# The gate products of the two gated mixers run one weight tile ahead of the up products, with two places for the sigmoid and the merged rows' low halves in three pieces

## The reference, cut to what matters

```python
a = rms_norm(h, g_mix)
q, k, v, g_ret, cb, cc, ch, gate_r, gate_c = split(a @ w_in)
ret = silu(g_ret) * head_group_norm(chunkwise_retention(rotary(q), rotary(k), v))
y_ret = ret @ w_ret_up
z = causal_short_conv(cc * ch, conv_w, conv_b)
y_conv = (cb * z) @ w_conv_up
merged = sigmoid(gate_r) * y_ret + sigmoid(gate_c) * y_conv
h = h + merged @ w_out
h = h + peer_ffn(rms_norm(h, g_ffn), ...)     # queries, top-k of product keys, experts
ple = p @ w_ple_proj
h = h + sigmoid(rms_norm(h, g_ple) @ w_ple_gate) * ple
return rms_norm(h, g_final)
```

## Time and profile before

| what | value |
|---|---|
| time, median of 3 runs | 3687.8 us (3678.93 to 3694.53) |
| the profiled execution | 3681.89 us, of which the span is 3680.1 us |
| PE busy (matmul) | 3420.2 us, 93% |
| VectorE (DVE) busy | 2709.3 us, 74% |
| GpSimd (POOL) busy | 2170.0 us, 59% |
| ScalarE (ACT) busy | 1195.2 us, 32% |
| granted TensorE clock, mean | 0.966 |

### The profile page before, as it was taken

The page is one execution under the profiler, slowest core; times in us unless marked ns, Lnnn a source line. Parts: engine busy times, 40 slices in busy tenths (PEclk is TensorE's granted clock), DMA queues, the critical chain, the costliest instruction groups (busy, mean ns, idle before and its releaser), DMA issues. The chain is left out here.

```text
span 3680.1 us, 59182 instructions
## 1 busy us (share of the span) xinstructions
PE 3420.2 (93%) x22379; PEld 3353.9 (91%) x22379; DVE 2709.3 (74%) x4191; ACT 1195.2 (32%) x1855; POOL 2170.0 (59%) x1406
## 2 busy tenths in 40 slices
PE   7899978989999889899999999998999999989987
PEld 6799978989999789899999999997999999989965
DVE  5524368676886666998989898652888888888854
ACT  2310131232221233455656555542222222222232
POOL 5478755323687555566666666664666666656521
PEclk9999989999999899999999999998999999999998
DMA  4233322112688768788888888897988989979701
GB/s 150 81 114 122 130 97 69 61 48 74 230 312 304 257 217 280 250 314 291 314 293 307 305 307 308 320 345 248 316 307 304 315 314 317 323 267 325 244 18 63
DMA packets 324155, 851.86 MB, mean 231 GB/s; under 512 B 27536, under 2 KB 125328, under 8 KB 320656
## 3 DMA queue, kind: packets, MB, share of 16 engines
q0 software_dynamic: 110592, 402.70, 30.6%
q1 hardware_dynamic: 72864, 258.15, 20.5%
q10 hardware_dynamic: 140528, 188.78, 14.7%
HBM read 754.62 MB, written 94.90 MB: 231 GB/s over the span
## 5 line engine op out<-in xcount | busy, mean ns | idle before, releaser
L582 POOL TENSOR_TENSOR w_lo<-raw,w_hi 128x1024 fp32r<-128x1024 f32 x206 | 544.8, 2645 | 434.4 <-ACT w_hi L1017 430.6
L681 PE MATMUL main<-mix_hi,w_hi 128*128 128x320 f32 (+1 forms) x2816 | 689.9, 319 | 52.9 <-issue 17.1
L681 PE MATMUL main<-mix_lo,w_hi 128*128 128x320 f32 (+1 forms) x2816 | 677.2, 314 | 0.0
L681 PE MATMUL main<-mix_hi,w_lo 128*128 128x320 f32 (+1 forms) x2816 | 676.3, 314 | 0.0
L609 POOL DMA_INDIRECT rows<-v_rows,s_idx x384 | 391.4, 1019 | 335.2 <-DVE scr L1632 273.2
L681 PEld LDWEIGHTS main<-mix_hi,w_hi 128*128 128x128 f32 x2816 | 480.7, 191 | 57.8 <-issue 40.5
L1632 DVE SCALAR_TENSOR_TENSOR scr<-rows,s_dot,scr 128x1024 f32<-128x1024 f32 x381 | 487.9, 1281 | 45.1 <-DMA rows<-v_rows,s_idx 34.6
L926 PE MATMUL main<-h_hi,v_hi 128*128 128x320 f32 x2048 | 474.9, 313 | 38.0 <-DVE res L2022 20.8
L681 PE MATMUL main<-a_hi,w_hi 128*128 128x320 f32 (+1 forms) x1728 | 466.7, 324 | 34.4 <-POOL w_lo L582 18.2
L609 POOL DMA_INDIRECT rows<-u_rows,s_idx x384 | 390.2, 1016 | 162.3 <-DVE s_dot L1625 85.2
L681 PEld LDWEIGHTS main<-mix_lo,w_hi 128*128 128x128 f32 x2816 | 484.0, 191 | 0.0
(11 more groups left out here) (243 smaller groups left out, 5310.7 us busy)
## 6 DMA issues: line engine op xcount, KB each, us to landing
raw<-stream SPq DMA_DIRECT2D x474, 512.0 KB
act_d<-actb ACTq DMA_DIRECT2D x128, 320.0 KB
gate_d<-gbuf ACTq DMA_DIRECT2D x20, 2048.0 KB, 10.1
h<-act_d ACTq DMA_DIRECT2D x128, 320.0 KB
gate_in<-gate_d ACTq DMA_DIRECT2D x31, 1280.0 KB
rows<-u_rows,s_idx POOLq DMA_INDIRECT x384
rows<-v_rows,s_idx POOLq DMA_INDIRECT x384
score_d<-stage ACTq DMA_DIRECT2D x16, 320.0 KB
```

The lines of the kernel that those rows point to most:

```text
L582: pool.tensor_tensor(w_lo[:, s, :], raw[:, s, :], w_hi[:, s, :].bitcast(F32), ALU.subtract) \
L681: last = pe.matmul(main[s][:, dst:dst + n], wt[:, s, c * P:(c + 1) * P], rows[:, c, src:src + n], start=(c == 0 and wt is w_hi and rows is ...
```

## The change

The order of the 16 tiles of M1, and of M2, changes. Before, it was gate 0, up 0, gate 1, up 1 and so on. Now it is gate 0, gate 1, up 0, gate 2, up 1, ..., gate 7, up 6, up 7: gate n is tile 2n-1 (`gate_at`), up n is tile 2n+2 (`up_at`), but the last up is tile 15. The host lays the stream out so. All gates but the first go to `main[1]`, all ups but the last to `main[0]`. Since two sigmoids are alive at a time there is a second place, `sg_ahead`, by the parity of n. The loops of ScalarE and VectorE over the pairs are written out in pass 0 too. In M1 of pass 1 the exponentials of the sparse scores, the picks and the ranks keep their place between the pairs; `spare` is called one tile later in each pair. The low halves of the merged rows, seven in a row before the last merge until now, are made in pieces: rows 0 to 3 after gate 7 is done and before merge 6, rows 4 to 6 after merge 6, row 7 after merge 7. The casts of the high halves stay where they were in ScalarE's queue, behind all sigmoids and, in pass 1, behind the weight casts of M2.

```diff
@@ SBUF
-        nt0, rowb, sg, pbuf, z = [], [], [], [], []
+        nt0, rowb, sg, sgs, pbuf, z = [], [], [], [], [], []
...
+                ahead = lay(f"sg_ahead{k}", [P, w], F32)
+                sgs.append((sg[k], ahead))
@@ TensorE, mixers
-                of_mix(base + M1_PAIR, 1, ready=2 * DC * ps)
-                with pe.Fori(1, DC) as n:
-                    of_a(base + M1_PAIR + n, 0)
-                    of_mix(base + M1_PAIR + n, 1)
+                of_a(base + M1_PAIR, 1)
+                of_mix(base + M1_PAIR + 1, 0, ready=2 * DC * ps)
+                of_a(base + M1_PAIR + 1, 1)
+                with pe.Fori(2, DC - 1) as n:
+                    of_mix(base + M1_PAIR + n, 0)
+                    of_a(base + M1_PAIR + n, 1)
+                for s in range(2):
+                    of_mix(base + M1_PAIR + DC - 1, s)
...
                 of_a(base + M2_PAIR, 0)
+                of_a(base + M2_PAIR, 1)
                 pe.wait_ge(z_used, DC * ps + DC + 1)
-                of_mix(base + M2_PAIR, 1)
...
@@ ScalarE, mixers
-                def gate(tile, merged):
+                def gate(first, n, merged):
+                    tile = 2 * first + gate_at(n)
                     act.wait_ge(tile_done, tile + 1)
-                    act.wait_ge(merged_done, merged)
...
+                    act.wait_ge(merged_done, merged + max(n, 1))
+                    act.activation(alike(sgs[ps][n % 2][:, :], ps), cols(main[tile % 2], ps), ACT.Sigmoid) \
+                        .then_inc(main_drained[tile % 2], 1)
+
+                def gates(first, merged, between=lambda at: None):
+                    for at in range(2 * DC):
+                        if at == 0 or at % 2 and at < 2 * DC - 1:
+                            gate(first, (at + 1) // 2, merged)
+                        if ps:
+                            after(first + at // 2, at % 2)
+                        between(at)
@@ VectorE, mixers
+                def up_product(first, n, out):
+
+                    g, u = 2 * first + gate_at(n), 2 * first + up_at(n)
+                    dve.wait_ge(main_drained[g % 2], g // 2 + 2)
+                    dve.wait_ge(tile_done, u + 1)
+                    dve.tensor_tensor(alike(out, ps), cols(main[u % 2], ps), alike(sgs[ps][n % 2][:, :], ps),
+                                      ALU.mult).then_inc(main_drained[u % 2], 1)
+                    dve.wait_ge(main_drained[u % 2], u // 2 + 2)
...
                 def merge(n):
...
+                    r, sgn = res_row(n, ps), sgs[ps][n % 2][:, :]
+                    if n < DC - 1:
+                        spare(2 * M2_PAIR + up_at(n) - 1)
+                    up_product(base + M2_PAIR, n, sgn)
+                    steps.then(dve.tensor_tensor(r, r, sgn, ALU.add))
                     dve.sem_inc(merged_done, 1)
...
+                    if n < DC - 2:
+                        spare(2 * M2_PAIR + up_at(n))
...
-                dve.wait_ge(tile_done, 2 * (base + M2_PAIR + DC - 1) + 1)
-                lo_of(ps, 2 * DC, a_lo[ps], a_hi[ps], range(DC - 1))
+                for n in range(DC - 2):
+                    merge(n)
+                dve.wait_ge(tile_done, 2 * (base + M2_PAIR) + gate_at(DC - 1) + 1)
+                lo_of(ps, 2 * DC, a_lo[ps], a_hi[ps], range(4))
+                merge(DC - 2)
+                lo_of(ps, 2 * DC, a_lo[ps], a_hi[ps], range(4, DC - 1))
                 merge(DC - 1)
@@ host
-    for n in range(DC):
-        parts += [gc[n], up_c[n]]
+    parts += ahead(gc, up_c)
```

More of the change, by code:

```diff
@@ L132, in tile_of, with gate_at, up_at @@
     return LEAD + SPAN * (m // 16) + QUARTERS[m % 16]
+def gate_at(n):
+    return 2 * n - 1 if n else 0
+def up_at(n):
+    return min(2 * n + 2, 2 * DC - 1)
 def row_homes():
@@ L1138, in mixers @@
                         act.copy(row_of(mix_hi[ps], 2 * i + k), z[ps][:, :]).then_inc(z_hi, 1)
-                with act.Fori(0, DC) as n:
-                    gate(2 * (base + M2_PAIR + n), done + 2 * DC + n + 1)
-                    if ps:
-                        for s in range(2):
-                            after(base + M2_PAIR + n, s)
+                gates(base + M2_PAIR, done + 2 * DC)
                 for c in range(DC):
@@ L1836, in mixers @@
                 if ps == 0:
-                    with dve.Fori(0, DC) as n:
+                    for n in range(DC):
                         gated(n)
@@ L1844, in mixers @@
                         steps.leave(inside, DC // 2)
-                    with dve.Fori(0, DC - 1) as n:
-                        inside = steps.enter(n, 1)
-                        merge(n)
-                        steps.leave(inside, DC - 1)
                 else:
```

63 lines of the change are left out of this document (20 added, 43 removed).

## The result

The changed kernel takes 3697.1 us, median of 20 runs, against 3687.2 us for 20 runs of before: a ratio of 1.0028, 95% interval 1.0019 to 1.0037. The sign is right, and so is the forecast that the two kernels lie within 0.5% of each other.

The account below looks back on a forecast made before the run. PE, busy 93% of the span, bounds the kernel, so only edges count: 0 + 1.9 + 0.3 - 0.4 + 5.8 - 1 = +6.6 us on 3687.8 gives 3694.4 us, range 3682 to 3703.

Parts of the forecast that it names:

- What bounds the kernel: PE works 93% of the span; nothing to win inside M1 and M2, so the change acts at the edges only.
- M1 begins, pass 0: Start of M1, pass 0: wait for `mix_lo` becomes a like wait for the sigmoid; 0 us, bounds -2.3 and +1.4.
- it ends at 186.09 + 0.49 = 186.58: M1, pass 0: end of gate 0's sigmoid, so up 0 starts 2.1 us later than before.
- M1 begins, pass 1: Start of M1, pass 1: idle joins into one wait of about 7 us, then lower clock; +1.9 us, bounds 0 and +2.
- C begins, pass 1: Start of C, pass 1: last pick and `s_idx` late, partly covered; +0.3 us, bounds 0 and +1.3.
- M2, pass 0: Pass 0: convolution wait at M2's start goes, -0.4 us; M2's end gains little as VectorE and GpSimd take turns, -1.
- M2 ends, pass 1: End of M2, pass 1: low halves wait for `a_hi`, three dots and merge 6 follow; +5.8 us, bounds +5.2 and +8.
- (a): Rival: low-half pieces work in both passes, last `a_hi` casts 5.2 and 5 us earlier; 3679.4 us, chance 0.1.
- (b): Rival: the loss at M2's end in pass 1 is hidden in the `x_t` loads; 3688.6 us, chance 0.1.
- (c): Rival: gather ring stops GpSimd inside M2 too, up to 3 us for each of six merges; 3712 us, chance 0.05.

Follow-up runs that it names:

- held kernels: GpSimd's two halves of M1's fourth tile, pass 0, held until row 6's cast: changed kernel 3691.48 us (single execution); with all edges 3663.25 us.
- piece of seven: Changed kernel with pass 1's low halves in one piece again, behind merge 6; pass 0 keeps its pieces: 3688.24 us, ratio 1.0002.
- all edges: Changed kernel, pass 1: three dots before low halves, row casts early, M1's first weight cast and sigmoid early, dots before `x_t` wait: 3665.75 us, ratio 0.9947.
- empty hold: GpSimd's halves of M1's fourth tile, pass 0, held until row 4's cast, already made: changed kernel 3695.3 us; with all edges 3669.98 us.

## Why the prediction was right

**What bounds the kernel: right.** PE has no wait inside M1 or M2 in either pass; over 1116 to 1216 us of after it is busy without a gap. All that moved lies at the edges.

**M1 begins, pass 0: forecast 0, measured +2.6; the step that failed.** The mechanism that I named is there: up 0 waits for the sigmoid (the profile calls it issue: PE starts at 191.37, 0.1 us after the sigmoid's end), and the matmuls behind it start at the lower level. What failed is "it ends at 186.09 + 0.49 = 186.58". I moved PE's tiles and let ScalarE's and VectorE's times stand. But gate 1 in up 0's place ends 7.7 us sooner and frees GpSimd's halves sooner, which meet VectorE's two `y`. I had reasoned just so at the end of M2 in pass 0, and did not ask it here. Its size is 3.89 - 1.03 = 2.9 us, and the held kernels give 3.0 back. PE was then at the lower level for 12 matmuls where I had counted 15, which took 0.4 us off. The upper bound of +1.4 did not hold the 2.6 us.

**M1 begins, pass 1: forecast +1.9, measured +2.55.** One wait of 6.78 us for w_lo, as laid out. PE starts at the lower level, 0.53 us from pair to pair in place of 0.29, for 11 pairs, where I had counted 9 and 2.0 us; 11 x 0.24 = 2.6. The term was mis-sized, the mechanism right. One part of it I had not seen: before, PE was at the lower level too after its first wait there, for 12 matmuls,

```profile
827.63 0.90 PE L681 MATMUL main<-mix_hi,w_hi 128*128 128x320 f32 x2 [2.53 <-DVE mix_lo L1657]
```

but the second wait, to 835.47, stood behind them and covered them. So PE's idle time was not only moved together; it grew from 5.1 to 6.8 us, since the tiles ahead of it now run fast, and what costs time is that the slow start now stands behind the last wait.

**C begins, pass 1: forecast +0.3, measured -0.1.** I had put `s_idx` at 1.5 to 3.3 us late, and that did not come: it is made 4.5 us behind the first copy of C, where it was 4.3, and the first gather follows at 5.8, where it was 5.6. The instruction that makes it takes 0.29 us, where it took 1.29 beside a low half on GpSimd; how the rest of the delay went is not worked out. PE has no wait there: the lower of my bounds.

```profile
952.36 1.11 POOL L621 DMA_INDIRECT rows<-u_rows,s_idx  x1 [1.65 <-DVEq L1615]
```

**M2, pass 0: forecast -0.4 and -1, measured -1.9.** The 0.4 us wait is gone. VectorE and GpSimd take turns as I had laid out:

```profile
413.80 5.04 DVE L1675 TENSOR_TENSOR a_lo<-res,a_hi 128x384 fp32r<-128x384 f32 x4 [3.58 <-ACT a_hi L1164]
418.76 0.55 DVE L1778 TENSOR_TENSOR sg<-main,sg 128x384 f32<-128x384 f32 x1
419.34 2.17 DVE L1834 TENSOR_TENSOR res<-res,sg 128x384 f32<-128x384 f32 x1
421.66 4.27 DVE L1675 TENSOR_TENSOR a_lo<-res,a_hi 128x384 fp32r<-128x384 f32 x3 [0.15 <-DVE res L1834]
```

Seven low halves take 9.3 us, where one piece took 8.58, and the add between them 2.17 in place of 0.56. From M2's first sigmoid to the last cast it is 427.08 - 357.81 = 69.3 us, before 423.49 - 353.46 = 70.0: -0.8. The other 1.1 us lie behind the last cast (39.3 us to the end of the stage before, 38.1 after): the 2.2 us wait for the first `add_out` went, since PE ran slow just where it would have waited. That 1.1 us is luck: with M1's old order the same code, with the clock up a little longer, has the wait again.

The Trainium skill (SBUF — State Buffer, "Who interferes with whom") makes the port pair that VectorE and GpSimd share an exclusive lock. The trace agrees: two products `y` go from 1.03 to 3.89 us, in pass 1 from 1.56 to 3.66. Of the seven low halves above, the three that meet no GpSimd instruction, or start just ahead of one, take 0.55 to 0.57 us, and the four that meet one 1.16 to 2.76, each until 0.4 us behind its end.

**M2 ends, pass 1: forecast +5.8, measured +6.9 for the stage and +6.0 from the last weight cast to the second tile of O.** Line by line: four low halves 3.03, dots to 1229.25, merge 6 with the add at 1.23 against a low half on GpSimd, three low halves 2.30, merge 7 ended 1235.37. That is 12.5 us from the first low half, and I had 12.2. Of the other 0.9 us of the stage 0.75 lie behind the start of the second tile of O (56.56 us to the end of the stage, before 55.81): PE is at the lower level for 21 steps there where it was for 15, though its wait is the shorter one. The slow start of the first tile costs nothing, as I had said, since the second wait stands behind it. That the whole piece of seven brings back the old stage shows what was added to the path; that the early casts take another 8.0 us off, on top of the dots, shows that ScalarE's queue held the pieces there.

**The rivals.** (a) is out in the change as it stands: the idle before the first low half is put down to `a_hi`, and with the casts moved, and the dots first, its pass 1 comes true. (b) is out: the wait for `x_t` is 9.14 us, it was 8.79. The loads moved with the cast by their full amount. (c) is out: no wait inside M2. That the sum came to +6.6 against +10.1 is the 2.6 us of M1 in pass 0, 1.1 at the end of M2 and 0.65 in M1 of pass 1, less 0.5 in pass 0 and 0.4 in C. That the forecast lies only 2.7 us off in time is in part luck: the medians differ from before's by 9.9 us in one measurement (20 runs of after) and by 5.4 in the other (12).

## What to carry to other kernels

When a step is moved between engines that work in order, go through the queue of every engine that feeds it, not only the one that was edited: here low halves were cut in pieces for VectorE while their casts stayed behind a weight cast on ScalarE, and the pieces put three dots and a merge on the path. Six casts moved two places forward, with the dots first, turned the same edit from a loss of 6.9 us in its stage into a gain of 6.5. And when a wait has independent work queued behind it, do that work first: one call ahead of a wait for loads gave the kernel before 10.8 us in that stage, without any reordering.

## What the runs showed of the hardware

A product or subtraction of VectorE with two operands in SBUF, 128x384, takes 0.55 us alone, 1.2 to 1.4 when it meets GpSimd's cast of a weight tile and 2.2 to 2.8 when it meets the subtraction. Which of them meet depends on which product ended first, so a change in PE's order can cost on engines that it doesn't name. Holding GpSimd back by 3.5 us gave 3.0 back.

PE starts a weight tile's matmuls at the lower level after a wait of 3.69 us, as after one of 15.6, but also after waits of 1.84, 2.19 and 2.53 us (before, at 421.45, 431.85 and 827.63). After 2.55 us (before, 835.47), 2.77 (one piece of seven) and 2.03 (all edges) it starts at the higher. A slow start costs nothing when another wait stands behind it, as at 827.63, and its full length behind the last one: 2.6 us in M1 of pass 1. After three waits of 0.20, 1.33 and 1.39 us (421.34 to 428.24) it fell in after and not with M1's old order, whose waits are the same to 0.01 us: what the engine waited did not alone decide it.

The parts of the program that nobody edited scatter, by 5 us ahead of the mixers and by 11 behind, from one execution to the next. And the four kernels with the hold, empty or not, have the stretch between the passes 2 to 3 us longer, M1 of pass 1 1.1 us shorter and M2 and O of pass 1 0.9 to 1.8 shorter than their counterparts, though their code is the same there but for a loop on GpSimd that is cut in two. For M1 the trace has the difference in the clock: after the same wait of 6.8 us PE is at the lower level for 12 matmuls with the empty hold, where it is for 21 in after. The rest stays open; it is the size below which a stage's difference between two programs of different shape should not be explained.
